# Spreading the gates with strided factors: one column order for both, the whole widening on ScalarE

## The reference

```python
expert = i1 * PEER_NKEYS + i2
gate = jax.nn.softmax(best, axis=-1)
...
act = jax.nn.gelu(jnp.einsum('td,thkd->thk', tc, u_sel).astype(jnp.float32), approximate=False)
return jnp.einsum('thk,thkd->td', (act * gc).astype(tc.dtype), v_emb[ec])
```

## Time and profile before

| | us |
|---|---|
| median of 3 runs | 3801.01 (3787.31 to 3805.46) |
| the profiled execution, its own time | 3802.57 |
| its span in the trace | 3800.8 |
| `spread_gates`, from its first comparison to its last copy-out | 1420.2 to 1704.7 |
| TensorE busy over the span | 3240.3 (85%) |
| VectorE busy over the span | 2361.9 (62%) |
| ScalarE busy over the span | 943.5 (25%) |

### The profile page before, as it was taken

The page is one execution under the profiler, slowest core; times in us unless marked ns, Lnnn a source line. Parts: engine busy times, 40 slices in busy tenths (PEclk is TensorE's granted clock), DMA queues, the critical chain, the costliest instruction groups (busy, mean ns, idle before and its releaser), DMA issues. The chain is left out here.

```text
span 3800.8 us, 47440 instructions
## 1 busy us (share of the span) xinstructions
PE 3240.3 (85%) x17309; PEld 2547.8 (67%) x17309; DVE 2361.9 (62%) x5002; ACT 943.5 (25%) x1346; POOL 987.5 (26%) x877
## 2 busy tenths in 40 slices
PE   8997998999665516554999999999999999999995
PEld 4444666764544405544999988888788888788883
DVE  2122333433499989992888877777677777544443
ACT  2212333421111105651222222222222222222221
POOL 0000000000023230001333335555555555322221
PEclk9996778889887859996999999999999999999998
DMA  4112101100200003547777779999989999665655
GB/s 182 47 61 92 22 17 45 33 28 23 93 25 25 13 1 89 156 124 270 246 259 247 257 254 357 351 350 351 346 341 356 351 350 352 244 232 218 220 210 197
DMA packets 326827, 706.20 MB, mean 186 GB/s; under 512 B 72432, under 2 KB 165872, under 8 KB 325104
## 3 DMA queue, kind: packets, MB, share of 16 engines
q0 software_dynamic: 110592, 402.70, 29.3%
q1 hardware_dynamic: 211328, 295.76, 22.4%
q10 hardware_dynamic: 4720, 5.26, 0.4%
HBM read 632.86 MB, written 70.78 MB: 185 GB/s over the span
## 5 line engine op out<-in xcount | busy, mean ns | idle before, releaser
L1514 PE MATMUL psum<-hn_hi_e,u_hi 128*128 128x320 f32 x2048 | 635.0, 310 | 59.3 <-DMA hn_lo_e<-scr_lo 55.7
L1514 PE MATMUL psum<-hn_hi_e,u_lo 128*128 128x320 f32 x2048 | 635.1, 310 | 0.0
L1514 PE MATMUL psum<-hn_lo_e,u_hi 128*128 128x320 f32 x2048 | 635.0, 310 | 0.0
L1498 POOL DMA_INDIRECT v_ring<-v_rows,eidT x384 | 441.0, 1148 | 698.4 <-PE psum L1557 591.9
L1530 PE MATMUL psum<-v_hi,w_hi 128*128 128x512 f32 x1280 | 511.3, 399 | 10.9 <-DVE coefT L1687 8.9
L1664 DVE TENSOR_TENSOR res<-psum,res 128x512 f32<-128x512 f32 x640 | 434.3, 688 | 123.9 <-PE psum L1530 123.9
L1530 PE MATMUL psum<-v_lo,w_hi 128*128 128x512 f32 x1280 | 501.2, 392 | 0.0
L1530 PE MATMUL psum<-v_hi,w_lo 128*128 128x512 f32 x1280 | 499.7, 390 | 0.0
L1491 POOL DMA_INDIRECT res<-u_rows,eid x288 | 338.6, 1176 | 385.7 <-DVE dots L1675 325.1
L1514 PEld LDWEIGHTS psum<-hn_hi_e,u_hi 128*128 128x128 f32 x2048 | 386.6, 189 | 64.8 <-DMA hn_lo_e<-scr_lo 55.9
L1644 DVE TENSOR_TENSOR w<-psum,w 128x640 f32<-128x640 f32 x128 | 105.6, 825 | 482.6 <-ACT psum L1597 482.6
(11 more groups left out here) (221 smaller groups left out, 4794.4 us busy)
## 6 DMA issues: line engine op xcount, KB each, us to landing
u_raw<-uT SPq DMA_DIRECT2D x128, 512.0 KB, 5.8
v_raw<-v_rows SPq DMA_DIRECT2D x128, 512.0 KB, 6.8
scr_g<-gates SPq DMA_DIRECT2D x5, 8192.0 KB, 30.5
w<-scr_g SPq DMA_DIRECT2D x128, 320.0 KB, 4.5
scr_m<-st_m SPq DMA_DIRECT2D x8, 1024.0 KB, 3.8
w_raw<-in_w_pq SPq DMA_DIRECT2D x8, 1024.0 KB, 5.5
w_in<-in_w_in SPq DMA_DIRECT2D x3, 2048.0 KB, 15.6
scr_a<-st_a SPq DMA_DIRECT2D x8, 768.0 KB, 3.2
```

The source lines that it names most:

```text
L1498: pool.indirect_dma_start(v_ring[:, m % V_RING, :], None, core.i["v_rows"], bass.IndirectOffsetOnAxis(eidT[:, m // P, t:t + 1], 0)).then_i ...
L1514: last = nc.tensor.matmul(ps[:, a, 0:COLS], x[:, c, j, :], y[:, j, a * COLS:(a + 1) * COLS], start=m == 0, stop=m == len(terms) - 1)
```

## The change

`first` and `second` take the order of `one1` and `one2`, key then token. So VectorE's product writes side by side, and ScalarE widens all eight tokens with one plain copy. VectorE's copy (line 1299) and its semaphore go. TensorE reads column t of each factor with a step of eight f32 elements, 32 bytes, for the weights and for the moving operand alike. The sizes, the number of matmuls, the number of buffers and the output to PSUM stay.

```diff
-        first = sb("first", [P, BUFS, OCT, NKEY])
-        second = sb("second", [P, BUFS, OCT, NKEY])
+        first = sb("first", [P, BUFS, NKEY, OCT])
+        second = sb("second", [P, BUFS, NKEY, OCT])
...
-                need(dve, second_act, n - BUFS + 1)
+                need(dve, second_ready, n - BUFS + 1)
                 need(dve, first_ready, n - BUFS + 1)
-                need(dve, second_dve, n - BUFS + 1)
...
                 nc.vector.tensor_tensor(
-                    first[:, b, :, :].rearrange("p t i -> p i t"), one1[:, b, :, :],
+                    first[:, b, :, :], one1[:, b, :, :],
                     flat[:, 2, n * OCT:(n + 1) * OCT].rearrange("p (o t) -> p o t", o=1)
                     .to_broadcast([P, NKEY, OCT]), ALU.mult).then_inc(first_ready, 1)
-                dve.wait_ge(ones_ready, n * 2 + 2)
-                nc.vector.tensor_copy(second[:, b, ON_ACT:, :], one2[:, b, :, ON_ACT:].rearrange("p i t -> p t i")
-                                      ).then_inc(second_dve, 1)
...
                 pe.wait_ge(first_ready, n + 1)
-                pe.wait_ge(second_act, n + 1)
-                pe.wait_ge(second_dve, n + 1)
+                pe.wait_ge(second_ready, n + 1)
...
-                    last = nc.tensor.matmul(slot, first[:, b, t, :], second[:, b, t, :], start=True, stop=True)
+                    last = nc.tensor.matmul(slot, first[:, b, :, t], second[:, b, :, t], start=True, stop=True)
...
-                nc.scalar.activation(second[:, b, 0:ON_ACT, :], one2[:, b, :, 0:ON_ACT].rearrange("p i t -> p t i"),
-                                     ACT.Copy).then_inc(second_act, 1)
+                nc.scalar.activation(second[:, b, :, :], one2[:, b, :, :], ACT.Copy).then_inc(second_ready, 1)
```

More of the change, by code:

```diff
@@ L1239, in spread_gates @@
     NOCT = TD // OCT
-    ON_ACT = 4
     with ExitStack() as ctx:
@@ L1252, in spread_gates @@
         iota_ready, keys_ready = sem("iota_ready_g"), sem("keys_ready_g")
-        ones_ready, first_ready, second_act, second_dve = (sem(x) for x in (
-            "ones_ready", "first_ready", "second_act", "second_dve"))
+        ones_ready, first_ready, second_ready = sem("ones_ready"), sem("first_ready"), sem("second_ready")
         spread_done, gates_out = sem("spread_done"), sem("gates_out")
```

## The result

The changed kernel took 3831.9 us (median of 20 runs), the kernel before 3799.7 (20 runs). The ratio is 1.0089, interval 1.0055 to 1.0122. Some executions of a kernel take over 1.5% longer than its fastest; the ratios in this document leave them out. The forecast was 3711, which is faster than before; the range that went with it, 3700 to 3860, holds the measured time. Of the rivals, the one in which a hop costs TensorE what it costs the other engines gave 3815 to 3831.

What follows compares the result with a forecast made beforehand. The prediction took VectorE to bound the stretch of 80 groups at 3.51 us each. Going to 2.35 saves 93 us, the start gives 2 back: -91, so 3711 us, 2.4% faster, range 3700 to 3860.

Steps and rivals of the forecast that it cites:

- the one in which a hop costs TensorE what it costs the other engines: Weight loads and matmuls of each group: 3.67 to 3.87 us a group, 3815 to 3831 us in all; chance 0.30.
- What bounds the stretch, and that it reaches the end whole: 80 groups between two barriers: VectorE sets 3.51 us a group, and any saving or loss reaches the end whole.
- VectorE's copy goes, the product gets 1.14: VectorE's group: copy of 0.52 us removed, product from 1.79 to 1.14 us without hops, group 2.35 us.
- ScalarE's widening costs nothing: ScalarE widens eight tokens in 0.96 us, about 2.0 with the copy-out, hidden in a group of 2.35.
- The slow start costs 2 us: Block's opening, TensorE's clock at 0.50: its first 32 instructions take 6.80 us, VectorE's two groups 4.7; about 2 lost once.
- TensorE's stepped read costs nothing: Weights and moving operand read with 32-byte steps: instructions stay 116 ns apart, 1.86 us a group, VectorE sets 2.35.
- the end above it: TensorE's stepped reads at VectorE's or ScalarE's hop price, 1.72 or 1.82 ns: 3.67 or 3.87 us a group.
- Both reasons for the lower end: For free stepped reads: fp32r matmuls reach 0.49 ns a column; stepped PSUM writes stand 116 ns apart against 112.
- the sign turns at 219.5 ns: Distance of TensorE's instructions, 1.64 ns a column, from which the change was said to be slower than before.
- The rival of adding streams: Weight load and matmul hops add up: 475 ns an instruction, 7.6 us a group, +327 us, 4130; chance 0.15.
- The rival of the unchanged product: VectorE's product stays at 1.79 us, only the copy goes: 2.99 us a group, -42 us, 3761; chance 0.05.
- The rival in which TensorE pays in part (150 to 204 ns): TensorE's stepped reads: 2.4 to 3.27 us a group, up to -20 us, around 3750; chance 0.10.

Runs made afterwards that it cites:

- second 8-byte profile: Against the changed kernel, both factors stored in token pairs so TensorE steps by 8 bytes; run again, ratio 0.973 to the kernel before.
- 8-byte kernel: Against the changed kernel, both factors stored in token pairs so TensorE steps by 8 bytes; ratio to the kernel before 0.983, then 0.973.
- 12-byte weights: Against the changed kernel, token pairs with three words a key in the weights, moving operand stepping 8 bytes; 2.77 us a group.

## Why the prediction was wrong, point by point

- **What bounds the stretch, and that it reaches the end whole:** right. +26.0 us in the stretch gave +26.8 in the span; -93.5 (the second 8-byte profile) gave -91.5.
- **VectorE's copy goes, the product gets 1.14:** right. The product's record is 1226 ns after the change against 1222 forecast from other contiguous rows, and it was the hop that had cost the time: with the same types and the same broadcast gate the product takes 2.02 us with hops and 1.23 without. Where TensorE is out of the way (8-byte steps), a VectorE group is 2.34 us against 2.35 forecast.
- **ScalarE's widening costs nothing:** right. It takes 1.05 us in the changed kernel, where ScalarE waits 1.86 us a group; and in the 8-byte kernel, where VectorE sets the pace, TensorE's gap still ends with VectorE's product.
- **The slow start costs 2 us:** this term was too large. In the 8-byte kernel, which has the forecast's rhythm, VectorE waited for TensorE's first group once, 0.37 us. In the changed kernel the term does not arise, since TensorE sets the pace from the start. Its first 36 instructions took 8.96 us, 244 ns apart, at a mean granted clock of 0.68 in the window from 1424 to 1428 (0.50, the lower level, until 1426 and 1.00 from 1427) and 1.00 afterwards:

```profile
1424.00:1428.00 4.00, 4.00 (x19) 0.68 0.00 0
1428.00:1432.00 4.00, 4.00 (x18) 1.00 0.00 0
...
1423.29 8.96 PE L1305 MATMUL psum<-second,first 128*128 128x128 f32 x36 [6.83 <-DVE first L1291]
```

  19 and 18 instructions in the two windows: while the lines set the pace, the clock does not. Side by side the distance did go with the clock, 0.21 us over the first 32 instructions against 116 ns later.
- **TensorE's stepped read costs nothing: this step failed.** The prediction took the lower of its two ends. It measured 240 ns an instruction; the end above it, from the hops of the two other engines, was 229 to 242. With 240 in place of 116 a group takes 3.83 us on TensorE instead of 2.35 on VectorE, and 80 x 1.48 = 118 us is the way from the forecast -91 to the measured +26.8. Both reasons for the lower end were of the wrong kind. The surplus seen in fp32r matmuls is one of words that lie side by side: 0.49 ns a column is 1.97 ns for four columns, and so for a line. The objection stood in the text of the rival, and it fits what was measured. And that writes to PSUM with 16-byte steps are nearly free (116 against 112 ns) says nothing of reads from the other memory: reads with that very step take 236.
- **The rival's conditions:** the sign turns at 219.5 ns; 240 is beyond it. Its sum for 242 ns was +29 us; the trace has +26.8.
- **The rival of adding streams:** refuted, 238 and 233 ns alone, 240 together, where it had 475. **The rival of the unchanged product:** refuted, 1226 ns. **The rival in which TensorE pays in part (150 to 204 ns):** not at 32 bytes; the 12-byte weights gave such a price, 173 ns.

What decided the sign was thus one price that no row of the trace showed. Two other engines' prices for the same kind of access (1.72 and 1.82 ns) were a better guide to it (1.80) than the surplus of the engine itself.

## What to carry to other kernels

When a layout moves the hop from one engine to another, count it where it lands. For TensorE that is how many 16-byte lines each instruction touches, at the 1.7 to 1.8 ns a line measured here, against what the instruction takes now. There can be an order in between. Pairs of f32 tokens side by side let VectorE write at its full rate (1219 ns against 1226), ScalarE nearly so (1.13 us against 1.05) and TensorE read nearly so (123 ns against 116), where each of the pure orders charges one side for every element. And where two engines share a price for a kind of access, reckon with it for a third until a row shows otherwise.

## What the runs showed of the hardware

- The hops of TensorE's weight loads and of its moving operand overlap: with a step of 32 bytes in either the instructions are 233 to 238 ns apart, with it in both 240.
- The distance with hops does not follow TensorE's clock: 244 ns over the start, with the mean granted clock still at 0.68 in one window, and 240 at 1.00.
- ScalarE widens 1024 elements in 1.05 us when it writes them side by side, in about 1.13 when it writes runs of two words, and in 2.1 when it reads with hops.
- VectorE's product takes 1219 to 1272 ns with runs of two words that start on 8 bytes, and 1341 with 12-byte steps, where every second run starts on an odd word and every fourth crosses a line; which of the two costs the time is open. Why VectorE's rows in the second 8-byte profile are longer than in the first (1272 against 1219 ns) is open too.
- Four columns of fp32r at 0.49 ns or less are a line in under 2.0 ns. Whether the fp32r matmuls, the greater part of TensorE's work in this kernel, also run at the memory's pace is open.
